# Residual rows kept in SBUF, expert weights two blocks ahead, and a last stage reordered over tiles, in a one-layer decoder step

## The chip, the cores and the metric

The kernel runs on one core of one Trainium2 chip. The metric is the device time of one execution in microseconds (us). Engines are named as the profile names them: PE (TensorE matmul), PEld (TensorE weight load, which overlaps PE), DVE (VectorE), ACT (ScalarE), POOL (GpSimd) and SP (SyncE, which here only issues transfers).

## What is computed

One decoder layer over 1,024 prompt rows, 16 meta rows and 8 sample rows (1,048 rows of 1,024 float32 values): attention and a gated recurrence are mixed, projected and added to the input, and a mixture of experts follows. Only the last part is touched by the change.

```python
x = x + (sigmoid(gm) * o_mla + sigmoid(gg) * o_gdn) @ w_out       # output projection
hf = rms_norm(x, norm_ffn)
eid, ew = hier_route(hf, w_group, b_group, w_router, b_router)    # 2 of 32 experts a row
x = x + moe_experts(hf, eid, ew, w_gate, w_up, w_down)
y = rms_norm(x, norm_final)

def moe_experts(h, expert_id, weight, w_gate, w_up, w_down):
    # rows are sorted by expert and padded to blocks of 128 slots per expert
    def expert_block(args):
        tok, e = args
        xb = h[tok]
        return (silu(xb @ w_gate[e]) * (xb @ w_up[e])) @ w_down[e]
    y = lax.map(expert_block, (slot_tok.reshape(n_blocks, 128), blk_expert))
    y = y.reshape(n_slots, -1) * slot_w[:, None]
    return zeros_like(h).at[slot_tok].add(y)
```

Each expert has w_gate and w_up of 1024x256 and w_down of 256x1024, 1 MB each. All values are float32. A matmul of float32 operands leaves two weight-load and two matmul records in the trace; a transpose leaves one of each.

## The kernel before

Stages follow each other, each a block of instruction streams for the five engines that meet only in semaphores, with a barrier between stages. The four last stages are `project_output`, `route`, `experts` and `combine`. Rows are handled in nine tiles: a first of 24 rows and eight of 128.

`project_output` (line 2139). SP issues `w_out` in two halves by output columns (`load_w`, line 2173), with the first part of the mixed activations `mix` between them (`load_mix`, line 2177), then input rows, norms, router weights and the two other parts of `mix`. For each tile PE makes 16 matmuls of 512 columns into `acc` (line 2241), DVE adds them to the rows `x` (2266), ACT squares and sums (2296), DVE and ACT make the root, DVE scales (2276) into `h`. `x` has two buffers, so POOL stores each tile of `x` to the HBM tensor `resid` (2204) and `h` to `ffn_in` (2205), and SP loads the rows of tile t+2 only after the stores of tile t (2196).

`route` (2304) computes for each row its two experts and two slots, and fills `slot_token`, the list of rows by slot. Unused slots hold token 0. It also gives `block_expert` (the expert of each block of 128 slots) and `turns`.

`experts` (2439). Blocks 0 and 1 stand before a loop of two blocks a turn, one block behind it. There are 33 blocks in use. Per block b: POOL gathers its 128 rows of `ffn_in` into `x[i]` (2531); PE turns them with eight transposes (2550), ACT and DVE copy them to `xT` (2590). For w_gate and then w_up PE makes eight matmuls (2561) with `xT` stationary (128x128) and 256 columns of weights moving; the result `gu` has slots on partitions. ACT takes silu (2604), DVE multiplies into `h` (2622), PE turns `h` with two transposes (2569), ACT copies them to `hT` (2610), and PE makes four matmuls of 512 columns with w_down (2577). ACT and DVE copy the result to `y`, which SP stores to `expert_out` (2510). PE does the transposes of block b+1 between line 2561 and line 2569 of block b. The weights have two buffers. SP issues all three transfers of block b+1 (2501 to 2503) when the w_down matmuls of block b-1 are done (`y_done`), from the start of body(b).

`combine` (2635). SP loads three tiles of `resid` ahead (2655) and one after each stored tile; POOL gathers two rows of `expert_out` per output row (2677), three tiles ahead. Per tile, in this order, DVE adds the first and second weighted rows (2688, 2690), waits for ACT's sum of squares (2706), makes mean and reciprocal (2692, 2694), waits for ACT's root (2708) and scales (2698); SP stores the tile (2665).

In rows a matmul reads "out<-moving,stationary": `ex_gu<-ex_wg,ex_xT` moves `ex_wg` through `ex_xT`.

## Time and profile before

| | us |
|---|---|
| median of 3 runs | 2903.77 (2901.22 to 2904.08) |
| the profiled execution | 2902.68 |
| its span | 2901.0 |
| project_output | about 2166 to 2332 |
| route | about 2332 to 2382 |
| experts | about 2382 to 2836 |
| combine | about 2836 to 2901 |

The profiled execution lasts 1.7 us longer than its span and lies 1.1 us under the median of the runs. Stage limits are read from the first transfers that each stage issues. Times in rows are us from the start of the span, "mean ns" is one instruction, and a bracket says how long the engine was idle before and what released it.

### The profile page before, as it was taken

How to read it: one execution, taken by the hardware profiler on the slowest of the kernel's cores; microseconds unless marked ns; L12 is line 12 of the kernel's file. 1: busy time of each engine (PE TensorE's matmuls, PEld its weight loads, DVE VectorE, ACT ScalarE, POOL GpSimd, SP SyncE). 2: the span in 40 equal slices, each digit the busy share in tenths (PEclk: the TensorE clock that was granted, in tenths of full speed). 3: DMA queues.
4: the chain of work that ended last, by engine and by line, in shares of the span. 5: the costliest groups of instructions: out<-in, count | busy, mean ns of one | idle time of the engine just before them, and what ended most of it. 6: DMA issues, size and time to landing. Idle time of an engine off the chain costs nothing. (4 is left out here: it accounts for less than half of the span.)

```text
span 2901.0 us, 45934 instructions
## 1 busy us (share of the span) xinstructions
PE 2483.2 (86%) x18544; PEld 1903.7 (66%) x18544; DVE 1151.5 (40%) x2059; ACT 852.5 (29%) x1798; POOL 654.5 (23%) x698
## 2 busy tenths in 40 slices
PE   5999999997999967499999995999969919999980
PEld 5999999997888854255655664565644516666660
DVE  6366563221566634345445552443421121111115
ACT  3257731111233320244444451343311101111111
POOL 0220000000455532232233303344400030000002
PEclk9999999998899985799999996999979959999995
DMA  4562223222633211400001005465614217888867
GB/s 128 168 215 85 79 96 118 89 83 93 192 103 107 64 39 59 159 1 23 23 31 38 23 9 197 174 258 217 243 42 169 80 65 303 318 321 332 314 265 250
DMA packets 180001, 404.16 MB, mean 139 GB/s; under 512 B 32275, under 2 KB 116984, under 8 KB 158921
## 3 DMA queue, kind: packets, MB, share of 16 engines
q1 hardware_dynamic: 144649, 245.65, 24.5%
q0 software_dynamic: 35168, 155.88, 14.8%
q8 instruction: 137, 2.24, 0.3%
q14 instruction: 47, 0.39, 0.0%
HBM read 310.76 MB, written 90.92 MB: 138 GB/s over the span
## 5 line engine op out<-in xcount | busy, mean ns | idle before, releaser
L131 PE MATMUL pi_acc<-hT_hi,pi_w_hi 128*128 128x352 f32 (+1 forms) x1152 | 378.3, 328 | 0.0
L131 PE MATMUL pi_acc<-hT_lo,pi_w_hi 128*128 128x352 f32 (+1 forms) x1152 | 371.3, 322 | 0.0
L131 PE MATMUL pi_acc<-hT_hi,pi_w_lo 128*128 128x352 f32 (+1 forms) x1152 | 371.2, 322 | 0.0
L131 PEld LDWEIGHTS pi_acc<-hT_hi,pi_w_hi 128*128 128x128 f32 x1152 | 217.2, 189 | 4.0 <-issue 3.8
L131 PEld LDWEIGHTS pi_acc<-hT_lo,pi_w_hi 128*128 128x128 f32 x1152 | 217.0, 188 | 4.0 <-issue 3.8
L131 PEld LDWEIGHTS pi_acc<-hT_hi,pi_w_lo 128*128 128x128 f32 x1152 | 216.9, 188 | 0.0
L1605 PE MATMUL at_sc<-at_keyT,at_qT 96*128 96x512 f32 (+5 forms) x480 | 162.7, 447 | 1.7 <-ACT at_val L1772 0.8
L1925 PE MATMUL as_tp<-ident,as_lat 128*128 128x128 f32 x1024 | 128.8, 281 | 25.4 <-ACT as_cT L2113 25.4
L1784 ACT ACTIVATE at_p<-at_sc,at_nm 16x16 f32<-16x16 f32 (+5 forms) x144 | 100.8, 700 | 160.0 <-DVE at_nm L1692 158.8
L1690 DVE TENSOR_REDUCE at_mx<-at_sc 16x1 f32<-16x16 f32 (+5 forms) x144 | 101.4, 704 | 99.2 <-PE at_sc L1609 98.0
L2241 PE MATMUL po_acc<-po_w,po_mix 128*128 128x512 f32 (+1 forms) x288 | 126.8, 599 | 14.0 <-DMA po_mix<-mixT 14.0
L1925 PEld LDWEIGHTS as_tp<-ident,as_lat 128*128 128x128 f32 x1024 | 113.3, 143 | 36.7 <-ACT as_cT L2113 28.9
L2577 PE MATMUL ex_yps<-ex_wd,ex_hT 128*128 128x512 f32 x264 | 122.1, 605 | 15.2 <-ACT ex_hT L2610 15.2
L2561 PE MATMUL ex_gu<-ex_wg,ex_xT 128*128 128x256 f32 x528 | 122.3, 385 | 13.5 <-DMA ex_wd<-w_down 9.7
L1623 PE MATMUL at_tp<-ident,at_p 128*128 128x128 f32 (+2 forms) x720 | 111.5, 286 | 26.1 <-ACT at_pT L1762 16.9
L2561 PEld LDWEIGHTS ex_gu<-ex_wg,ex_xT 128*128 128x128 f32 x528 | 100.0, 192 | 47.0 <-issue 34.6
L124 DVE TENSOR_SCALAR pi_m<-pi_piece 128x768 int32<-128x768 int32 (+1 forms) x72 | 40.9, 568 | 221.9 <-PE pi_acc L131 149.7
L1623 PEld LDWEIGHTS at_tp<-ident,at_p 128*128 128x128 f32 (+2 forms) x720 | 78.6, 138 | 75.4 <-issue 33.8
L651 ACT ACTIVATE pi_xr<-pi_acc 128x352 f32<-128x352 f32 x144 | 57.9, 472 | 235.4 <-PE pi_acc L131 235.4
L2113 ACT COPY as_cT<-as_tp 128x512 f32<-128x512 f32 x160 | 92.1, 586 | 98.7 <-PE as_tp L1925 98.7
L2561 PE MATMUL ex_gu<-ex_wu,ex_xT 128*128 128x256 f32 x528 | 119.3, 379 | 0.0
L1636 PE MATMUL at_op<-at_pT,at_val 128*64 128x128 f32 (+2 forms) x1440 | 114.0, 301 | 0.6 <-ACT at_pT L1762 0.6
(477 smaller groups left out, 4654.1 us busy)
## 6 DMA issues: line engine op xcount, KB each, us to landing
ex_wg<-w_gate SPq DMA_DIRECT2D x33, 1024.0 KB
ex_wu<-w_up SPq DMA_DIRECT2D x33, 1024.0 KB
ex_wd<-w_down SPq DMA_DIRECT2D x33, 1024.0 KB
pi_piece<-w_in SPq DMA_DIRECT2D x64, 384.0 KB, 3.4
expert_out<-pi_zero POOLq DMA_DIRECT2D x33, 512.0 KB, 12.0
expert_out<-ex_y SPq DMA_DIRECT2D x33, 512.0 KB, 2.7
projT<-pi_xr POOLq DMA_DIRECT2D x24, 524.0 KB, 3.0
convT<-pi_yn POOLq DMA_DIRECT2D x24, 512.0 KB, 2.9
```

What stands on the lines that cost most here:

```text
L131: last = nc.tensor.matmul(out, lhs[a], rhs[b], start=(start and i == 0), stop=(stop and i == 2))
L651: last = nc.scalar.activation(xr[:, u % XR, a0:a1], ps, func)
L1605: last = nc.tensor.matmul(scf[0:n, x:e], qT[0:QK, slot, r0:r0 + n], keyT[:, slot, x - base:e - base], start=True, stop=False, skip_group_c ...
L1623: last = nc.tensor.transpose(tp[0:kn, g % 2, j - groups[g][1], 0:n], p[0:n, u % 3, k0:k0 + kn], k.ident[0:n, 0:n])
L1636: last = nc.tensor.matmul(op[a * NOPE:(a + 1) * NOPE, 0:n], val[0:kn, j, h * NOPE:(h + 1) * NOPE], pT[0:kn, w % 2, a, j, 0:n], start=(j == ...
L1690: nc.vector.reduce_max(mx[0:n, i:i + 1], scf[0:n, base:base + kl], AX_X).then_inc(maxed, 1)
L1784: nc.scalar.activation(p[0:n, u % 3, 0:kl], scf[0:n, base:base + kl], ACT.Exp, bias=nm[0:n, i:i + 1], scale=MLA_SCALE, accum_out=l[0:n, i: ...
L1925: last = nc.tensor.transpose(tp[:, g % 3, r * P:(r + 1) * P], mine, k.ident[:])
L2113: nc.scalar.copy(cT[:, half, c, :], tp[:, g % 3, :]).then_inc(kept_a, 1)
L2241: last = nc.tensor.matmul(acc[0:n, t % 2, b, :], mix[:, c, r0:r0 + n], w[:, c, b * BANK:(b + 1) * BANK], start=(c == 0), stop=(c == KD - 1))
L2561: last = nc.tensor.matmul(gu[:, i, j, :], xT[:, i, c, :], w[:, i, c * DE:(c + 1) * DE], start=(c == 0), stop=(c == KD - 1))
L2577: last = nc.tensor.matmul(yps[:, n, :], hT[:, i, c, :], wd[:, i, c * D + n * BANK:c * D + (n + 1) * BANK], start=(c == 0), stop=(c == KE - 1))
```

## The change

- Rows of `x` stay in one SBUF tensor `resid_rows` (nine tiles, 36 KB a partition) from `project_output` to `combine`. The stores to `resid` and the loads from it are gone. The input rows of tiles 2 to 8 come in one transfer behind `mix`.
- `w_out` comes in eight parts of 512 KB (two of eight row blocks, one half of the columns), behind the first part of `mix`; tile 0 waits for them one by one.
- Unused slots of `slot_token` hold 65536. The gather gets a bound of 1047 and skips rows beyond it; the two `x` buffers are cleared by POOL first. DVE limits partition 0 of the index to 1047, so that at least one row of each block is fetched.
- In `experts` the operands of the w_gate and w_up matmuls change places: the weights are stationary, 128 of 256 columns at a time, every second one (`w[:, i, c * DE + e:(c + 1) * DE:KE]`), and the 128 slots of `xT` move. `gu` then has expert columns on partitions, DVE's product is `hT` itself, and the two transposes and ACT's copy of them are gone.
- SP issues w_gate and w_up of block b+2 when the w_gate and w_up matmuls of block b are done (`gu_done`), and w_down of block b+2 at `y_done` of block b. The expert's number is read before the wait. Two blocks stand ahead of the loop and three behind it.
- In `combine` DVE works on two tiles in turn (`normalise`, `scale`), and ACT's root comes one tile later (`root`).

PE's order in one block of `experts`, first before, then after the change; `ex_xps` are the transposes of the next block.

```order
L2561 MATMUL ex_gu<-ex_wg,ex_xT 128x256 x8
L2561 MATMUL ex_gu<-ex_wu,ex_xT 128x256 x8
L2550 MATMUL ex_xps<-ident,ex_x 128x128 x8
L2569 MATMUL ex_hps<-ident,ex_h 128x128 x2
L2577 MATMUL ex_yps<-ex_wd,ex_hT 128x512 x4
```

```order
L2568 MATMUL ex_gu<-ex_xT,ex_wg 128x128 x16
L2568 MATMUL ex_gu<-ex_xT,ex_wu 128x128 x16
L2556 MATMUL ex_xps<-ident,ex_x 128x128 x8
L2578 MATMUL ex_yps<-ex_wd,ex_hT 128x512 x4
```

Sixteen matmuls of 256 moving columns have become 32 of 128, and the line with `ex_hps` is gone.

DVE's order in `combine`, in the middle of the stage, first before, then after. `co_r` and `resid_rows` are the rows that are added to.

```order
L2688 SCALAR_TENSOR_TENSOR co_r<-co_y,weight,co_r 128x1024
L2690 SCALAR_TENSOR_TENSOR co_r<-co_y,weight,co_r 128x1024
L2692 TENSOR_SCALAR co_mean<-co_ss 128x1
L2694 RECIPROCAL co_inv<-co_mean 128x1
L2698 SCALAR_TENSOR_TENSOR co_out<-co_r,co_rstd,co_nf 128x1024
```

```order
L2690 SCALAR_TENSOR_TENSOR resid_rows<-co_y,weight,resid_rows 128x1024
L2674 TENSOR_SCALAR co_mean<-co_ss 128x1
L2676 RECIPROCAL co_inv<-co_mean 128x1
L2694 SCALAR_TENSOR_TENSOR resid_rows<-co_y,weight,resid_rows 128x1024
L2683 SCALAR_TENSOR_TENSOR co_out<-resid_rows,co_rstd,co_nf 128x1024
```

The mean, the reciprocal and the scaling now belong to the tile before the one that is being added.

The diff, cut to its core:

```diff
+NO_TOKEN = 1 << 16
...
-        x, h = s.sb("po_x", [P, 2, D]), s.sb("po_h", [P, 2, D])
+        x, h = k.resid, s.sb("po_h", [P, 2, D])
...
-                load_w(0)
                 load_mix(0)
-                load_w(1)
-                load_x(0)
-                load_x(1)
+                for i in range(4):
+                    load_w(0, i)
+                for i in range(4):
+                    load_w(1, i)
+                sp.dma_start(x[0:NS, 0, :], d["x_sample"].rearrange("b t d -> (b t) d")).then_inc(x_loaded, 16)
+                sp.dma_start(x[NS:HEAD_ROWS, 0, :], d["meta_tokens"]).then_inc(x_loaded, 16)
+                sp.dma_start(x[:, 1, :], d["x_prompt"][0, 0:P, :]).then_inc(x_loaded, 16)
...
-                for t in range(2, NT):
-                    sp.wait_ge(stored[t % 2], 32 * (t // 2))
-                    load_x(t)
+                sp.dma_start(x[:, 2:, :], d["x_prompt"][0, P:, :].rearrange("(t p) n -> p t n", p=P)).then_inc(rows_loaded, 16)
...
-                    pool.dma_start(d["resid"][r0:r0 + n, :], x[0:n, t % 2, :]).then_inc(stored[t % 2], 16)
                     pool.dma_start(d["ffn_in"][r0:r0 + n, :], h[0:n, t % 2, :]).then_inc(stored[t % 2], 16)
...
-                        if t == 0:
-                            pe.wait_ge(w_loaded[b], 16)
                         for c in range(KD):
+                            if t == 0 and c % 2 == 0:
+                                pe.wait_ge(w_loaded[b][c // 2], 16)
...
-                    dve.wait_ge(x_loaded[i], 16 * (t // 2 + 1) + (16 if i == 0 else 0))
+                    if t < 2:
+                        dve.wait_ge(x_loaded, 48)
+                    else:
+                        dve.wait_ge(rows_loaded, 16)
...
-                nc.gpsimd.memset(zero[:], 0).then_inc(cleared, 1)
+                nc.gpsimd.memset(zero[:], NO_TOKEN).then_inc(cleared, 1)
...
-                link(V.tensor_scalar(k.turns[:], incl[0:1, EXPERTS - 1:EXPERTS], -2.0, None, ALU.add))
+                link(V.tensor_scalar(k.turns[:], incl[0:1, EXPERTS - 1:EXPERTS], -4.0, None, ALU.add))
...
+            more = eng.value_load(k.turns[0:1, 0:1], min_val=(2 * ROWS // P - 4) // 2, max_val=TURNS)
+            body(0, 0, 2)
+            body(1, 1, 2)
             with eng.Fori(0, TURNS) as i:
-                with eng.If(i < busy):
-                    body(i * 2 + 2, 0, False)
-                    body(i * 2 + 3, 1, False)
-            body(busy * 2 + 2, 0, True)
-            return busy
+                with eng.If(i < more):
+                    body(i * 2 + 2, 0, 2)
+                    body(i * 2 + 3, 1, 2)
+            body(more * 2 + 2, 0, 2)
+            body(more * 2 + 3, 1, 1)
+            body(more * 2 + 4, 0, 0)
+            return more
...
-                def load(b, i):
-                    if not fixed(b) or b >= 2:
-                        sp.wait_ge(y_done, b - 1)
+                def load(b, i, before):
+                    e = sp.value_load(k.block_expert[0:1, bass.ds(b, 1)], min_val=0, max_val=EXPERTS - 1)
+                    if before is not None:
+                        sp.wait_ge(gu_done, before + 1)
                         sp.sem_inc(load_due, 1)
-                    e = sp.value_load(k.block_expert[0:1, bass.ds(b, 1)], min_val=0, max_val=EXPERTS - 1)
                     sp.dma_start(wg[:, i, :], wg_d[bass.ds(e, 1)].rearrange("e p n -> p (e n)")).then_inc(w_loaded[i], 16)
                     sp.dma_start(wu[:, i, :], wu_d[bass.ds(e, 1)].rearrange("e p n -> p (e n)")).then_inc(w_loaded[i], 16)
+                    if before is not None:
+                        sp.wait_ge(y_done, before + 1)
+                        sp.sem_inc(load_due, 1)
                     sp.dma_start(wd[:, i, :], wd_d[bass.ds(e, 1)].rearrange("e p n -> p (e n)")).then_inc(w_loaded[i], 16)
 
-                def body(b, i, last_one):
-                    if not last_one:
-                        load(b + 1, 1 - i)
+                def body(b, i, ahead):
+                    if ahead > 1:
+                        load(b + 2, i, b)
                     sp.wait_ge(y_kept_a, b + 1)
                     sp.wait_ge(y_kept_v, b + 1)
                     sp.dma_start(d["expert_out"][bass.ds(b * P, P), :], y[:, i].rearrange("p b n -> p (b n)")).then_inc(stored[i], 16)
 
...
+                load(0, 0, None)
+                load(1, 1, None)
+                more = turns(sp, body)
...
                     pool.sem_inc(gather_due, 1)
                     nc.gpsimd.indirect_dma_start(out=x[i][:], out_offset=None, in_=d["ffn_in"],
-                                                 in_offset=bass.IndirectOffsetOnAxis(ap=idx[i][:, 0:1], axis=0)).then_inc(gathered[i], 16)
+                                                 in_offset=bass.IndirectOffsetOnAxis(ap=idx[i][:, 0:1], axis=0),
+                                                 bounds_check=ROWS - 1, oob_is_err=False).then_inc(gathered[i], 16)
...
+                for i in range(2):
+                    nc.gpsimd.memset(x[i][:], 0.0).then_inc(x_cleared, 1)
+                pool.wait_ge(x_cleared, 2)
                 pool.wait_ge(slots_kept, 2)
...
                     for j, w in enumerate((wg, wu)):
-                        for c in range(KD):
-                            last = nc.tensor.matmul(gu[:, i, j, :], xT[:, i, c, :], w[:, i, c * DE:(c + 1) * DE], start=(c == 0), stop=(c == KD - 1))
+                        for e in range(KE):
+                            for c in range(KD):
+                                last = nc.tensor.matmul(gu[:, i, j, e * P:(e + 1) * P], w[:, i, c * DE + e:(c + 1) * DE:KE], xT[:, i, c, :], start=(c == 0), stop=(c == KD - 1))
                     last.then_inc(gu_done, 1)
-                    if not last_one:
+                    if ahead:
                         turn(b + 1, 1 - i)
                     pe.wait_ge(h_done, b + 1)
-                    if not fixed(b) or b >= 1:
-                        pe.wait_ge(h_kept, b)
-                    for c in range(KE):
-                        last = nc.tensor.transpose(hps[:, c, :], h[:, i, c:DE:KE], k.ident[:])
-                    last.then_inc(h_turned, 1)
-                    pe.wait_ge(h_kept, b + 1)
                     if not fixed(b) or b >= 1:
...
-                    act.wait_ge(h_turned, b + 1)
-                    if not fixed(b) or b >= 2:
-                        act.wait_ge(y_done, b - 1)
-                    nc.scalar.copy(hT[:, i], hps[:]).then_inc(h_kept, 1)
...
                     if not fixed(b) or b >= 2:
-                        dve.wait_ge(h_turned, b - 1)
-                    nc.vector.tensor_tensor(h[:, i, :], act_g[:, i, :], gu[:, i, 1, :], ALU.mult).then_inc(h_done, 1)
-                    if not last_one:
+                        dve.wait_ge(y_done, b - 1)
+                    nc.vector.tensor_tensor(hT[:, i].rearrange("p c t -> p (c t)"), act_g[:, i, :], gu[:, i, 1, :], ALU.mult).then_inc(h_done, 1)
...
-                nc.vector.tensor_copy(idx_all[:], hps[:, 0, 0:BLOCKS]).then_inc(slots_kept, 1)
+                nc.vector.tensor_copy(idx_all[:], hps[:, 0, 0:BLOCKS]).then_inc(idx_turned, 1)
+                dve.wait_ge(idx_turned, 1)
+                nc.vector.tensor_scalar(idx_all[0:1], hps[0:1, 0, 0:BLOCKS], float(ROWS - 1), None, ALU.min).then_inc(slots_kept, 1)
...
-        r, out = s.sb("co_r", [P, 3, D]), s.sb("co_out", [P, 3, D])
+        r, out = k.resid, s.sb("co_out", [P, 3, D])
...
-                def load(t):
-                    r0, n = TILES[t]
-                    sp.dma_start(r[0:n, t % 3, :], d["resid"][r0:r0 + n, :]).then_inc(r_loaded[t % 3], 16)
-
-                load(0)
-                load(1)
-                load(2)
...
-                    if t + 3 < NT:
-                        load(t + 3)
...
+                def normalise(t):
+                    i, n = t % 3, TILES[t][1]
                     dve.wait_ge(squared, t + 1)
                     nc.vector.tensor_scalar(mean[0:n, t:t + 1], ss[0:n, t:t + 1], 1.0 / D, EPS, ALU.mult, ALU.add).then_inc(meaned, 1)
                     dve.wait_ge(meaned, t + 1)
                     nc.vector.reciprocal(inv[0:n, t:t + 1], mean[0:n, t:t + 1]).then_inc(inverted, 1)
+
+                def scale(t):
+                    i, n = t % 3, TILES[t][1]
                     dve.wait_ge(rooted, t + 1)
                     if t >= 3:
                         dve.wait_ge(stored[i], 16 * (t // 3))
-                    nc.vector.scalar_tensor_tensor(out=out[0:n, i, :], in0=rt, scalar=rstd[0:n, t:t + 1], in1=nf[0:n, :], op0=ALU.mult, op1=ALU.mult).then_inc(normed, 1)
+                    nc.vector.scalar_tensor_tensor(out=out[0:n, i, :], in0=r[0:n, t, :], scalar=rstd[0:n, t:t + 1], in1=nf[0:n, :], op0=ALU.mult, op1=ALU.mult).then_inc(normed, 1)
+
+                dve.wait_ge(nf_loaded, 16)
+                for t, (r0, n) in enumerate(TILES):
+                    i = t % 3
+                    dve.wait_ge(gathered[i], 32 * (t // 3 + 1))
+                    rt = r[0:n, t, :]
+                    nc.vector.scalar_tensor_tensor(out=rt, in0=y[0][i][0:n, :], scalar=k.weight[0:n, 0, t:t + 1], in1=rt, op0=ALU.mult, op1=ALU.add).then_inc(half, 1)
+                    if t:
+                        normalise(t - 1)
+                    dve.wait_ge(half, t + 1)
+                    nc.vector.scalar_tensor_tensor(out=rt, in0=y[1][i][0:n, :], scalar=k.weight[0:n, 1, t:t + 1], in1=rt, op0=ALU.mult, op1=ALU.add).then_inc(added, 1)
+                    if t:
+                        scale(t - 1)
+                normalise(NT - 1)
+                scale(NT - 1)
...
                 for t, (r0, n) in enumerate(TILES):
+                    if t:
+                        root(t - 1)
                     act.wait_ge(added, t + 1)
...
-                    nc.scalar.activation(square[0:n, :], r[0:n, t % 3, :], ACT.Square, accum_out=ss[0:n, t:t + 1]).then_inc(squared, 1)
-                    act.wait_ge(inverted, t + 1)
-                    nc.scalar.activation(rstd[0:n, t:t + 1], inv[0:n, t:t + 1], ACT.Sqrt).then_inc(rooted, 1)
+                    nc.scalar.activation(square[0:n, :], r[0:n, t, :], ACT.Square, accum_out=ss[0:n, t:t + 1]).then_inc(squared, 1)
+                root(NT - 1)
...
+        k.resid = k.sb("resid_rows", [P, NT, D])
```

## Rows read from the trace of the kernel before

**Rows 1.** Window over experts: us; busy us (count) per engine; PEclk, DMA share, GB/s
```profile
2397.00:2832.00 435.00, 400.86 (x1642) 291.38 (x1642) 58.64 (x99) 64.05 (x133) 35.72 (x62) 1.00 0.78 306
```

**Rows 2.** Timeline of one block of experts: start us, us, engine, line, operation
```profile
2597.96 3.62 PE L2561 MATMUL ex_gu<-ex_wu,ex_xT 128*128 128x256 f32 x16
...
2601.41 1.05 PE L2550 MATMUL ex_xps<-ident,ex_x 128*128 128x128 f32 x8
...
2602.03 0.42 DVE L2622 TENSOR_TENSOR ex_h<-ex_act_g,ex_gu 128x256 f32<-128x256 f32 x1 [7.43 <-ACT ex_act_g L2604]
...
2602.51 0.51 PE L2569 MATMUL ex_hps<-ident,ex_h 128*128 128x128 f32 x2
...
2603.47 3.70 PE L2577 MATMUL ex_yps<-ex_wd,ex_hT 128*128 128x512 f32 x8 [0.46 <-ACT ex_hT L2610]
...
2607.01 3.62 PE L2561 MATMUL ex_gu<-ex_wg,ex_xT 128*128 128x256 f32 x16
```

**Rows 3.** Timeline, PE in experts: the same later, and its first and last block
```profile
2397.79 2.47 PE L2561 MATMUL ex_gu<-ex_wg,ex_xT 128*128 128x256 f32 x5 [0.88 <-DVE ex_xT L2590]
...
2610.46 3.62 PE L2561 MATMUL ex_gu<-ex_wu,ex_xT 128*128 128x256 f32 x16
...
2620.47 3.69 PE L2561 MATMUL ex_gu<-ex_wg,ex_xT 128*128 128x256 f32 x16 [0.63 <-DMA ex_wd<-w_down]
...
2818.64 3.71 PE L2561 MATMUL ex_gu<-ex_wg,ex_xT 128*128 128x256 f32 x16 [2.93 <-issue]
```

**Rows 4.** 128-column matmuls (timeline, x16); weight loads by line: ns min/median/max
```profile
821.77 1.95 PE L853 MATMUL gp_i<-gp_heads 128*128 128x128 f32 x16
...
L853 PEld LDWEIGHTS gp_i<-gp_heads x128: 190/192/192, 739.3 to 1018.2; 128*128 128x128 f32 x128
...
L844 PEld LDWEIGHTS gp_r<-ident,gp_heads x64: 139/141/146, 738.5 to 1016.4; 128*128 128x128 f32 x64
...
L2550 PEld LDWEIGHTS ex_xps<-ident,ex_x x264: 186/190/226, 2394.9 to 2810.6; 128*128 128x128 f32 x132
```

**Rows 5.** Waits in experts (us in total, times, longest); window at full DMA load
```profile
PE ex_gu L2561 <- DMA ex_wd<-w_down: 9.0, 14, 0.9
...
SPq L2509 <- DVE ex_y L2596: 336.9, 33, 25.0
...
2598.00:2603.00 5.00, 4.95 (x27) 4.17 (x25) 0.93 (x2) 0.89 (x2) 0.18 (x1) 1.00 0.99 415
```

**Rows 6.** Timeline of combine: first and last tile, and one in the middle on DVE
```profile
2845.69 1.27 DVE L2688 SCALAR_TENSOR_TENSOR co_r<-co_y,weight,co_r 24x1024 f32<-24x1024 f32 x1 [13.29 <-DMA co_y<-expert_out,dest]
...
2869.10 1.28 DVE L2688 SCALAR_TENSOR_TENSOR co_r<-co_y,weight,co_r 128x1024 f32<-128x1024 f32 x1
2870.42 1.28 DVE L2690 SCALAR_TENSOR_TENSOR co_r<-co_y,weight,co_r 128x1024 f32<-128x1024 f32 x1
...
2872.92 0.15 DVE L2692 TENSOR_SCALAR co_mean<-co_ss 128x1 f32<-128x1 f32 x1 [1.22 <-ACT co_square L2706]
...
2873.54 1.28 DVE L2698 SCALAR_TENSOR_TENSOR co_out<-co_r,co_rstd,co_nf 128x1024 f32<-128x1024 f32 x1 [0.27 <-ACT co_rstd L2708]
2874.74 1.28 DVE L2688 SCALAR_TENSOR_TENSOR co_r<-co_y,weight,co_r 128x1024 f32<-128x1024 f32 x1
...
2891.65 1.28 DVE L2688 SCALAR_TENSOR_TENSOR co_r<-co_y,weight,co_r 128x1024 f32<-128x1024 f32 x1
```

**Rows 7.** Windows: combine at its start and in its middle
```profile
2838.00:2845.00 7.00, 0.00 (x0) 0.00 (x0) 0.00 (x0) 0.00 (x0) 4.73 (x6) 0.50 0.99 284
2845.00:2880.00 35.00, 0.00 (x0) 0.00 (x0) 24.07 (x30) 9.39 (x19) 11.36 (x12) 0.50 0.92 328
```

**Rows 8.** Timeline and window of the start of project_output
```profile
2166.05 0.37 SPq L2175 DMA_DIRECT2D po_w<-w_out  x1
...
2175.92 16.56 PE L2241 MATMUL po_acc<-po_w,po_mix 128*24 128x512 f32 x34 [13.98 <-DMA po_mix<-mixT]
...
2170.00:2174.00 4.00, 0.00 (x0) 0.00 (x0) 0.00 (x0) 0.00 (x0) 0.00 (x0) 0.50 1.06 386
```

78 lines of the change are left out of this document (31 added, 47 removed).

## The prediction

> **What bounds the kernel now.** I read windows first to see which engine is full in which stage, then the timeline of one block or tile, then waits. The change touches three stages. In `experts` PE is busy 401 of 435 us at full clock, the transfers 0.78 of the time at 306 GB/s [rows 1], so PE and the chain that it waits for come first and transfers second. One block [rows 2]: from the w_up matmuls at 2597.96 to those of the next block at 2610.46 [rows 3] are 12.50 us. In them PE stands still only around the turning of `h`: 2602.51 the two transposes, 2603.47 the w_down matmuls, 0.96 us. Every second block is longer, since w_down of the next block has not landed: 9.0 us in 14 waits [rows 5], and 13.46 us from the start at 2607.01 to that at 2620.47. Over all blocks it is (2818.64 - 2397.79) / 32 = 13.15 us [rows 3]. In `combine` the chain DVE, ACT, DVE of each tile sets the pace: 5.64 us from 2869.10 to 2874.74 [rows 6], with transfers at 0.92 of the time and 328 GB/s [rows 7], so that they are not far behind. At the start of `project_output` PE waits 13.98 us, the last 9.87 of them for transfers issued from 2166.05 on [rows 8].
>
> The sum is made against the profiled execution, 2902.68 us, which is 1.1 us under the median of the runs; I add that at the end.
>
> **project_output.** Before, the first matmul needs 2 MB of w_out and 0.62 MB of mix. At the 386 GB/s of [rows 8] that is 7.0 of the 9.87 us, so 2.8 us are latency. After, it needs 0.62 + 0.52 MB: 3.0 + 2.8 = 5.8 us, 4 us earlier. The seven other parts take 1.4 us each; PE makes 34 matmul records in 16.56 us [rows 8], 0.49 us each, four to a part, so it asks for a part every 1.9 us and never waits. The rest of the stage is PE's, so the 4 us last to its end. The rows of tiles 2 to 8 (3.7 MB) stand last in SP's queue, behind some 9.6 MB: 34 us in all. DVE needs them when tile 2 is made, three tiles of 32 x 0.49 = 15.6 us after the first matmul, so they cost nothing. Bounds: 3 to 5. The smaller stores of POOL and the missing waits of SP cost and give nothing: DVE waits there for PE.
>
> **experts, the matmuls turned round.** Before, 32 records of 256 columns: 3.45 us for 16 [rows 2, 3], 0.216 each, 6.90 a block. After, 64 records of 128 columns, each with its own weight load. The nearest rows are contiguous float32 matmuls of this shape: 16 in 1.95 us [rows 4], the eight transposes in 1.05 us [rows 2], so eight more cost 0.90, 0.112 each. 64 x 0.112 = 7.17, 0.27 us more a block. This is the term on which all hangs, for the new stationary operand is read with a step of two elements, and no row has a float32 weight load with both its records at a step. What there is [rows 4]: contiguous loads last 192 ns for matmuls and 141 for transposes; the transposes of `ex_x`, read with a step of eight, 190. So a step costs a transpose 50 ns, and takes it to what a matmul's load has anyway. Two readings: a step only takes away something that transposes have and matmuls do not (spacing stays 0.112), or it doubles every load (spacing 0.215). I take the first, since 190 and 192 ns look like one floor, and the stepped transposes still follow each other at 0.11 us. The second is a rival.
>
> The Trainium skill, "SBUF — State Buffer", section "Door 1: The DMA port swizzle", says that SBUF has lines of 16 bytes and float32 can be read with a step of up to four elements at full rate. By that rule the load at a step of two costs nothing and the sum stays. No row here has that step on a weight load of a matmul, and a step of eight, which the rule charges, shows 190 against 141 ns.
>
> **experts, the chain.** Before, the last w_up matmul starts at 2597.96 + 15 x 0.216 = 2601.20, and the transposes of `h` 1.31 us later, released by DVE's product, which ends at 2602.45 [rows 2]. After, w_down's matmuls start there, and 0.11 earlier since the last matmul is 0.27 and not 0.38 us long: 1.20 us, of which the transposes of `x` fill 0.9. The 0.96 us for turning and copying `h` go. Next, w_down to the next block: 2607.01 - 2603.47 = 3.54, unchanged. A block: 63 x 0.112 + 1.20 + 3.54 = 11.80 us, 0.70 less than 12.50.
>
> **experts, weights two ahead.** The need per block is 3.1 MB of weights, 0.26 to 0.52 of gathered rows and 0.52 stored, 4.1 MB at most. At the 415 GB/s of a full window [rows 5] that is 9.9 us of 11.80, and each load has a whole block of slack, so the 0.88 us of every second block go (on average 0.44). SP's waits: the store of `y` now stands behind the wait for `y_done`, which comes before `y_kept` anyway, and the next w_gate stands behind the store; SP waits 336.9 us in this stage [rows 5], so nobody waits for it. The gather stands behind PE's transposes of the block before as it did, nine us ahead of its use.
>
> Sum: the first interval keeps its 1.6 us of half clock, the last its 3.1 us of empty loop turns (2.93 idle at 2818.64 [rows 3]). 31 intervals of 11.80, one of 14.9, plus 1.6 = 382.3, against 420.9 before: 38.6 less. The last block gives 0.7. The start: the first gather may be shorter by half, POOL's clears lie in its wait for the slot list, DVE's extra operation costs 0.2: 0 to 2, I take 0.7. Together 40 us, bounds 34 (a spacing of 0.115, a tenth of the blocks stalled) and 43.
>
> **combine.** First tile: 1.15 MB of `resid` no longer lie ahead of the gathers; at 284 GB/s [rows 7] 4.0 us, I take 3.5, since latency stays (0 to 4). Then DVE's work a tile: from the scaling to the next addition 1.20 (2873.54 to 2874.74), from addition to mean the same 1.20, mean and reciprocal 0.35, the second addition 1.24: 4.0 us against 5.64 [rows 6]. The wait of 1.22 us for the sum of squares and ACT's root now lie under other operations of DVE, the first addition and the second. What is late next is the transfers: 1.57 MB a tile, at 328 / 0.92 = 357 GB/s [rows 7] 4.4 us. Three tiles lie ready at the start, so I take 4.3. Eight intervals: 45.96 before (2845.69 to 2891.65 [rows 6]), 34.4 after, 11.6 less; with the start 15.1. The first of the eight intervals has no scaling and no mean in it yet, 2.6 us of DVE's work instead of 4.0; transfers allow about 1 us of that, so I take 16. Bounds: 8 (transfers at 328 GB/s, no gain at the start) and 19.
>
> **Sum.** 4 + 40 + 16 = 60: 2902.7 - 60 = 2842.7, and 1.1 for the median: **2844 us**.
>
> **The rivals.**
> - A, the sum above. Its own range is 2837 to 2856.
> - B, slower: the stepped weight load doubles. 64 records at 0.215 instead of 0.112 add 6.6 us a block, 33 blocks 218 us: 3062 us. It decides where the spacing passes 0.112 + 60 / 2112 = 0.140 us. For it speaks that a step visibly lengthens transposes' loads; against it, that the length ends at the matmul's own. Spacings between (0.16) give 2945.
> - C, transfers take the place of the chain: gathers, issued just after 2 MB of w_gate and w_up, land late, or w_down does. PE then waits as now, and blocks fall back to about 12.5 us: 31 x 0.7 = 22 us given back, 2866. For it: 9.9 of 11.8 us leaves little, and `combine` shows what mixed queues do to the rate (284 against 415 GB/s). Against: the slack of a whole block.
> - D, the change does not do what it says: the loads two ahead bring nothing because SP issues them late, blocks stay at alternating lengths. 31 x 0.44 = 14 us less gain, 2858. It falls in with C.
> - E, no difference. It needs a loss of 60 us at one place that is not B; I see none but a spacing near 0.14.
>
> **How the numbers follow.** A 0.70, B with its spacings between 0.14, C and D 0.12, faster than A (transfers lighter than I count, a start without waiting) 0.03, E 0.01. A measurement of this kernel can tell some 0.2%, 5.8 us, from no change. Faster by more than that: A, C, D and the faster case, 0.85. Slower: B, 0.14. Same: 0.01. The range takes in A, C, D and most of the faster case, 2832 to 2870; B, the other sign, lies outside with 0.14.
>
> **What would show each step.** Spacing of the records of `ex_gu`: 32 in about 3.6 us, or 6.9 in case B. Start of w_down's matmuls 1.2 us after the last of w_up, no wait on a copy of `hT`. Starts of w_gate's matmuls 11.8 us apart with no alternation and no wait on `ex_wd`; a wait on `ex_x` would be C. In `combine` 4.0 to 4.4 us between scalings on DVE; a wait on `co_y` means that transfers bind. First matmul of `project_output` 5.8 us after SP's first issue; a DVE wait on the rows of tiles 2 to 8 would break that step. The prediction is wrong at its root if the weight loads, 64 a block, last much more than 192 ns.

## The result and the profile after

The changed kernel takes 2858.52 us (median of 4 executions, 2857.41 to 2868.63) beside 2903.88 us for the kernel before on the same chip: a ratio of 0.9854, 95% interval 0.9831 to 0.9877. The forecast was 2844 us, range 2832 to 2870. The profiled execution took 2859.27 us with a span of 2857.6. That is 43.4 us less than before, where the sum of the prediction had 60.

To find where they went I cut each profiled execution at three marks: SyncE's first issue of `project_output`, the first w_gate matmul of `experts`, and SyncE's issue of `co_nf`, with which `combine` begins. Timeline of after at the three marks, with the row of before that has no group above:

```profile
2165.75 0.36 SPq L2174 DMA_DIRECT2D po_mix<-mixT  x1
...
2171.68 3.58 PE L2234 MATMUL po_acc<-po_w,po_mix 128*24 128x512 f32 x4 [10.05 <-DMA po_w<-w_out]
...
2393.36 5.65 PE L2568 MATMUL ex_gu<-ex_xT,ex_wg 128*128 128x128 f32 x32 [0.87 <-DVE ex_xT L2591]
...
2808.55 0.35 SPq L2650 DMA_DIRECT2D co_nf<-norm_final  x1
```

```profile
2836.35 0.35 SPq L2651 DMA_DIRECT2D co_nf<-norm_final  x1
```

| stage, us | before | after | gain | forecast |
|---|---|---|---|---|
| up to `project_output` (code unchanged) | 2166.05 | 2165.75 | 0.3 | 0 |
| `project_output`, `route`, to the first w_gate matmul | 231.74 | 227.61 | 4.1 | 4 + 0.7 |
| `experts`, to the issue of `co_nf` | 438.56 | 415.19 | 23.4 | 39.3 |
| `combine`, to the end | 64.65 | 49.05 | 15.6 | 16 |

Three of four stages came out as forecast; `experts` gave 15.9 us less. The total alone would not tell case A from rival D, which had 2858 us; the rows of `experts` do. One block of it in the timeline of after, to be read against [rows 2, 3], and the next start:

```profile
2554.20 3.92 PE L2568 MATMUL ex_gu<-ex_xT,ex_wg 128*128 128x128 f32 x32
2557.96 3.93 PE L2568 MATMUL ex_gu<-ex_xT,ex_wu 128*128 128x128 f32 x32
2561.73 1.04 PE L2556 MATMUL ex_xps<-ident,ex_x 128*128 128x128 f32 x8
2562.82 3.70 PE L2578 MATMUL ex_yps<-ex_wd,ex_hT 128*128 128x512 f32 x8
2566.36 3.92 PE L2568 MATMUL ex_gu<-ex_xT,ex_wg 128*128 128x128 f32 x32
2570.12 3.93 PE L2568 MATMUL ex_gu<-ex_xT,ex_wu 128*128 128x128 f32 x32
2573.89 1.04 PE L2556 MATMUL ex_xps<-ident,ex_x 128*128 128x128 f32 x8
2575.15 3.70 PE L2578 MATMUL ex_yps<-ex_wd,ex_hT 128*128 128x512 f32 x8 [0.22 <-DVE ex_hT L2619]
```

The reader is to see three things. Nothing waits for `ex_wd` any more. The 32 matmul records of w_gate take 2557.96 - 2554.20 = 3.76 us, 0.1175 us each and not 0.112. And the step from the transposes of `x` to w_down's matmuls is 1.09 us in one block and 1.26 in the next, so that starts of w_gate lie 12.16 and 12.33 us apart in turn, where 11.80 was forecast. The other differences are at the end of the loop. Timeline of after there, and windows. The first window is from the middle of the stage and has the busy time of all engines, as in [rows 1]; the other two have that of PE alone, then PEclk, DMA share and GB/s:

```profile
2765.37 5.56 PE L2568 MATMUL ex_gu<-ex_xT,ex_wg 128*128 128x128 f32 x32 [2.96 <-issue]
2770.76 3.93 PE L2568 MATMUL ex_gu<-ex_xT,ex_wu 128*128 128x128 f32 x32
```

```profile
2500.00:2600.00 100.00, 98.69 (x654) 81.65 (x654) 15.12 (x26) 13.31 (x26) 9.83 (x17) 1.00 0.90 323
...
2762.00:2766.00 4.00, 1.04 (x5) 0.96 1.01 335
2766.00:2770.00 4.00, 4.00 (x24) 0.61 0.88 308
```

The empty turns of the loop cost 2.96 us, as before the change (2.93, [rows 3]). But the w_gate matmuls behind them now take 5.56 us instead of 3.92, at a mean granted clock of 0.61 of 2.4 GHz, which is part of the time at 1.2 GHz. Before the change the same pause left the clock alone: 3.71 us [rows 3].

### The profile page after: what moved, and what is told of

The parts are those of the page before. It is cut to its first block and busy times, and to the rows that moved or that the text cites. A ratio compares the mean times of both kernels' runs of the same rounds, so it can differ in the third digit from the quotient of the medians.

```text
span 2857.6 us, 47826 instructions
## 1 busy us (share of the span) xinstructions
PE 2481.4 (87%) x19534; PEld 1940.6 (68%) x19534; DVE 1149.9 (40%) x2060; ACT 840.9 (29%) x1765; POOL 660.0 (23%) x691
## 5 line engine op out<-in xcount | busy, mean ns | idle before, releaser
L2568 PEld LDWEIGHTS ex_gu<-ex_xT,ex_wg 128*128 128x128 f32 x1056 | 132.6, 201 | 19.7 <-issue 19.7
L2568 PE MATMUL ex_gu<-ex_xT,ex_wg 128*128 128x128 f32 x1056 | 132.8, 286 | 3.8 <-issue 3.0
L1624 PE MATMUL at_tp<-ident,at_p 128*128 128x128 f32 (+2 forms) x720 | 111.5, 286 | 26.1 <-ACT at_pT L1763 16.9
L2568 PE MATMUL ex_gu<-ex_xT,ex_wu 128*128 128x128 f32 x1056 | 129.8, 281 | 0.0
L2568 PEld LDWEIGHTS ex_gu<-ex_xT,ex_wu 128*128 128x128 f32 x1056 | 127.0, 197 | 0.0
```

Of the source, the lines that this page charges most:

```text
L1624: last = nc.tensor.transpose(tp[0:kn, g % 2, j - groups[g][1], 0:n], p[0:n, u % 3, k0:k0 + kn], k.ident[0:n, 0:n])
L2568: last = nc.tensor.matmul(gu[:, i, j, e * P:(e + 1) * P], w[:, i, c * DE + e:(c + 1) * DE:KE], xT[:, i, c, :], start=(c == 0), stop=(c == ...
```

## Experiments

A table first, since it is what most of the runs are read by. All are profiled executions, cut at the same marks.

| run | up to `project_output` | to first w_gate | `experts` | `combine` | intervals of w_gate's starts |
|---|---|---|---|---|---|
| before | 2166.05 | 231.74 | 438.56 | 64.65 | 12.58 / 13.46 |
| after | 2165.75 | 227.61 | 415.19 | 49.05 | 12.16 / 12.33 |
| c2 contiguous slices | 2167.97 | 226.67 | 401.37 | 49.29 | 11.77 / 11.94 |
| c4 weights moving | 2168.44 | 228.08 | 426.55 | 49.83 | 12.50 / 12.67 |
| c5 loads one ahead | 2161.37 | 227.71 | 433.76 | 50.56 | 12.25 / 13.5 |
| c6 all rows gathered | 2165.60 | 227.63 | 415.31 | 51.36 | 12.16 / 12.32 |
| c7 combine in order | 2159.85 | 227.76 | 415.01 | 60.68 | 12.16 / 12.33 |
| c8 w_out in halves | 2165.00 | 231.45 | 415.07 | 47.78 | 12.16 / 12.32 |
| c9 loop to `more` | 2164.32 | 227.68 | 410.38 | 50.32 | 12.16 / 12.32 |
| c10 = c2 + c9 | 2162.12 | 226.43 | 398.54 | 50.41 | 11.77 / 11.94 |
| c11 = c10, waits, buffers | 2166.42 | 226.48 | 399.97 | 46.33 | 11.84 / 11.97 |
| c13 = c10, buffers | 2166.14 | 226.83 | 398.36 | 46.57 | 11.77 / 11.94 |

The first column is the same code in every row and differs by up to 8.6 us. `experts` has the same code in after, c7 and c8, and takes 415.01 to 415.19 us. So there a stage's own time resolves tenths of a microsecond where the whole resolves three or four, and where `experts` answers the question, I go by it. `combine` does not resolve as well: with the changed order and three buffers it takes 47.78 to 51.36 us in eight of these rows. Its gain of 15.6 us, from one execution of each kernel, could as well have been read as 13.3 to 16.9.

### c2: contiguous stationary slices

My theory of the missing 15.9 us: the weight loads of w_gate and w_up, read at every second element, are slower. The rival: matmuls are slowed by the transfers that now run beside all of them. To keep the result right the edit also lays w_down out anew, in two pieces of 4 KB per partition in place of one of 8 KB.

```
-wd_d = d["w_down"][0].rearrange("e (p c) n -> e p (c n)", p=P)
+wd_d = d["w_down"][0].rearrange("e (c p) n -> e p c n", p=P)
...
-  w[:, i, c * DE + e:(c + 1) * DE:KE]
+  w[:, i, c * DE + e * P:c * DE + (e + 1) * P]
```

> Stationary slices of w_gate and w_up contiguous (columns e*128 to e*128+127 of each chunk) instead of every second element; w_down is rearranged to match (row c*128+p, two pieces of 4 KB per partition instead of one of 8 KB), so the result is unchanged. Theory (the missing gain of the experts is the step of two): records of w_gate and w_up come 0.112 us apart instead of 0.118, the weight-load record takes 0.192 instead of 0.197, the interval between blocks falls from a mean of 12.25 to about 11.9, and the whole by 33 x 0.37 = 12 us, to about 2846. Rival (the matmuls are slowed by the transfers that now run beside all of them): spacing stays at 0.117 to 0.118 and the time at 2858. A second rival: 4 KB pieces make the w_down transfer later and a wait on ex_wd comes back, intervals 12.5 or more, 2865 or slower.

Measured: 2845.53 us, ratio 0.9814, interval 0.98 to 0.9828. Timeline of c2, a w_gate and a w_up pass, and the w_gate pass behind the pause:

```profile
2408.65 3.73 PE L2568 MATMUL ex_gu<-ex_xT,ex_wg 128*128 128x128 f32 x32
2412.22 3.74 PE L2568 MATMUL ex_gu<-ex_xT,ex_wu 128*128 128x128 f32 x32
...
2755.53 3.83 PE L2568 MATMUL ex_gu<-ex_xT,ex_wg 128*128 128x128 f32 x32 [2.92 <-issue]
```

3.57 us for 32, 0.112 each, exactly what the contiguous rows of [rows 4] had given; the transfers run beside as before (from 2500 to 2600 us at 336 GB/s and a share of 0.94, in after 323 and 0.90). The trace of after settles the rival too, and with it the other half of the edit. In its last block the passes are as long as in the middle, 3.76 us from w_gate's start to w_up's and 3.93 us for w_up's records, although no weights are being loaded any more: the queues move 131 GB/s from 2791 to 2795 us and nothing from 2795 to 2799. Timeline of after:

```profile
2791.49 3.92 PE L2568 MATMUL ex_gu<-ex_xT,ex_wg 128*128 128x128 f32 x32
2795.25 3.93 PE L2568 MATMUL ex_gu<-ex_xT,ex_wu 128*128 128x128 f32 x32
```

The weight loads by line, after first, then c2 (columns: busy us, mean ns):

```profile
L2568 PEld LDWEIGHTS ex_gu<-ex_xT,ex_wu 128*128 128x128 f32 x384 | 46.2, 197 | 0.0
```

```profile
L2568 PEld LDWEIGHTS ex_gu<-ex_xT,ex_wu 128*128 128x128 f32 x384 | 43.8, 192 | 0.0
```

197 ns against 192. The theory held, the rival is out: 0.39 us a block, 12.3 us in all. The other 1.5 of the 13.8 us by which `experts` is shorter in c2 is the pass behind the pause, 3.83 us where after had 5.56. The second rival, a late w_down in smaller pieces, did not come either.

### c3 and c12: steps of eight and of four

```
-  w[:, i, c * DE + e:(c + 1) * DE:KE]
+  w[:, i, e * 1024 + c:(e + 1) * 1024:8]
```

> Stationary slices of w_gate and w_up taken at every 8th element (32 bytes) instead of every 2nd; the values multiplied are then not the right columns, all else is unchanged. If a stepped weight load costs more as the step grows (the rival of the prediction by which a load doubles once it spans more lines of memory), spacing goes from 0.118 to 0.2 or more and the time from 2858 to 3030 or more; at the level of a load of twice the length (0.215) 33 x 64 x 0.097 = 205 us, 3063. If only being stepped at all costs, whatever the step, spacing stays 0.118 and the time 2858.

> Stationary slices of w_gate and w_up taken at every 4th element (16 bytes) instead of every 2nd; the values multiplied are then not the right columns, all else is unchanged. Steps of 1, 2 and 8 gave spacings of 0.112, 0.118 and 0.240 us. If a load is free up to a step of four elements (the rule of 16-byte lines as the Trainium skill has it) and only 0.006 us above a contiguous one as at two, spacing is 0.118 and the time 2858. If its cost grows with the span of memory that it covers, spacing lies between, near 0.15 to 0.18: 33 x 64 x 0.03 to 0.06 = 65 to 130 us more, 2920 to 2985.

(c12 differs from c3 in the step alone, 4 in place of 8.) Timelines, c3 first, then c12:

```profile
2511.75 7.69 PE L2568 MATMUL ex_gu<-ex_xT,ex_wg 128*128 128x128 f32 x32
2519.27 5.92 PE L2568 MATMUL ex_gu<-ex_xT,ex_wu 128*128 128x128 f32 x24
```

```profile
2512.37 7.50 PE L2568 MATMUL ex_gu<-ex_xT,ex_wg 128*128 128x128 f32 x32
2519.71 5.53 PE L2568 MATMUL ex_gu<-ex_xT,ex_wu 128*128 128x128 f32 x23
```

| step, elements (bytes) | us per record | whole, us |
|---|---|---|
| 1 (4) | 0.112 | 2846 |
| 2 (8) | 0.1175 | 2859 |
| 4 (16) | 0.229 | 3097 |
| 8 (32) | 0.235 | 3109 |

For eight I had given two outcomes without choosing, and the doubled one came, 46 us above its 3063. For four I had 0.118 or 0.15 to 0.18, and neither came. It is not the clock: from 2500 to 2600 us it was granted at 1.00 in both, and no wait for a transfer stands in either stage. The load records last 338 ns at a step of eight and 330 at four (median), against 197 at two and 192 contiguous. The cost does not grow in proportion to the span. It jumps to double between a step of two and one of four, and barely moves after that. So rival B, the doubled load, is real; this kernel stands one doubling of the step short of it, with two elements of every 16 bytes in use. A step of three was not run. One execution each is enough for 240 us.

### c4 and c5: the two halves of the change in experts

c4 turns the orientation back (w_gate and w_up moving, `h` transposed and copied) and keeps the loads two ahead; c5 does the reverse.

```
 c4:
-  last = nc.tensor.matmul(gu[:, i, j, e * P:(e + 1) * P], w[:, i, c * DE + e:(c + 1) * DE:KE], xT[:, i, c, :], ...)
+  last = nc.tensor.matmul(gu[:, i, j, :], xT[:, i, c, :], w[:, i, c * DE:(c + 1) * DE], ...)
 ...
+  last = nc.tensor.transpose(hps[:, c, :], h[:, i, c:DE:KE], k.ident[:])
 c5:
-  if ahead > 1: load(b + 2, i, b)
+  if ahead: load(b + 1, 1 - i)
```

> The changed kernel with the orientation of w_gate and w_up as before the change (weights moving, x stationary, h turned by two transposes and one copy), everything else of the change kept, loads two ahead too. Theory (terms add): no wait on ex_wd any more, interval 12.50 to 12.58 in every block, so the experts take 32 x 0.1 to 0.3 = 3 to 10 us more than in the changed kernel: 2862 to 2869. So the loads ahead are worth about 18 to 20 us and turning only 4 to 9. Rival (the loads ahead bring little, the turned orientation carried the gain): waits on ex_wd stay, intervals 12.6 / 13.4, 2885.

> The changed kernel with the weight loads one block ahead, as before the change (SyncE's order and waits of before), turned orientation and everything else kept. Theory: every second block waits for ex_wd again; the block that waits keeps its interval near 13.4 because the transfers set it and the other takes 12.2, mean 12.8, 32 x 0.55 = 18 us more than the changed kernel: 2876; if the pair of blocks is set by its transfers alone (26.0 for two), 13.0 and 2882. Rival (the loads ahead are worth nothing, since the halved gather freed the queues): no wait on ex_wd, intervals 12.2, 2858.

Measured: c4 2868.45 us, ratio 0.9888 (0.9873 to 0.9903); c5 2875.5 us, ratio 0.9919 (0.9904 to 0.9934). Both totals are within what the theory gave. The stage of c4 is not: its `experts` took 11.4 us more than in after, where the theory had 3 to 10, so turning is worth more beside early loads than I had put it. Timeline of c5, a block that waits, and waits of PE from 2410 to 2750 us (us in total, times, longest), in c5 and in after:

```profile
2507.16 4.01 PE L2564 MATMUL ex_gu<-ex_xT,ex_wg 128*128 128x128 f32 x32 [1.01 <-DMA ex_wd<-w_down]
...
PE ex_gu L2564 <- DMA ex_wd<-w_down: 14.2, 14, 1.3
```

```profile
PE ex_yps L2578 <- DVE ex_hT L2619: 3.1, 14, 0.2
```

| `experts`, us | loads one ahead | loads two ahead |
|---|---|---|
| weights moving | 438.56 | 426.55 |
| turned, step of two | 433.76 | 415.19 |
| turned, contiguous | not run | 401.37 |

The two halves do not add. Alone, turning brings 4.8 us and the loads 12.0; together 23.4. The reason stands in the waits: with loads one ahead a wait on `ex_wd` grew on average from 0.64 us (9.0 in 14 waits, [rows 5]) to 1.01 (14.2 in 14), so what PE saved in a waiting block went into the wait.

### c6: gathering all rows

```
-nc.gpsimd.memset(zero[:], NO_TOKEN)
+nc.gpsimd.memset(zero[:], 0)
...
-  bounds_check=ROWS - 1, oob_is_err=False
```

> The changed kernel, but empty slots of a block gather row 0 again instead of being skipped (slot list cleared with 0, no bounds on the gather), so the gathered bytes are those of before the change. Theory (the halved gather only makes transfers lighter, PE sets the interval): the experts move 0.25 MB more per block of 12.25 us, 21 GB/s on top of 323 at a share of 0.90; that stays under the full 359 GB/s (323 / 0.90), so intervals stay at 12.16 and 12.33 and the time at 2858 to 2860. Rival (the queues were just kept off the path by the smaller gather): waits on ex_wd or ex_x return, intervals 12.6 or more, 2870.

Measured: 2859.05 us, ratio 0.9848 (0.9824 to 0.9872). Windows of c6 in the middle of the stage:

```profile
2500.00:2600.00 100.00, 98.69 (x655) 81.68 (x654) 15.09 (x26) 13.28 (x26) 9.38 (x17) 1.00 0.95 341
```

`experts` takes 415.31 us instead of 415.19. Skipping empty slots brings the share from 0.95 to 0.90 and no time. The start gained nothing by it either: the first gather lands 9.1 us after its issue before and after the change (2381.45 to 2390.55).

### c7 and c8: combine in order, w_out in halves

```
 c7:
-  if t: normalise(t - 1)
...
-  if t: scale(t - 1)
+  normalise(t)
+  scale(t)
 c8:
-  load_mix(0)
-  for i in range(4): load_w(0, i)
-  for i in range(4): load_w(1, i)
+  load_half(0)
+  load_mix(0)
+  load_half(1)
```

> The changed kernel with VectorE's and ScalarE's order in combine as before the change (each tile is added, normalised and scaled before the next), rows still kept on chip. Theory: the start keeps its 4.3 us, the tile period goes back from 3.9 to 5.64, so of the 15.6 us of this stage 11 to 12 are lost: 2869 to 2871. Rival (the gain of the stage came from the residual loads that no longer share the queues, and transfers set the period): period 4.4 or less, 2862 or faster.

> The changed kernel with w_out loaded in two halves and mix between them as before the change, rows still kept on chip. Theory: first matmul of project_output 9.9 us after SyncE's first issue instead of 5.9, 4 us later, and all after it: 2862.5. Rival (the four microseconds are given back, since VectorE or the stores of ffn_in set the end of the stage): 2858.5.

Measured: c7 2870.42 us, ratio 0.9892 (0.9876 to 0.9908); c8 2860.69 us, ratio 0.9857 (0.9841 to 0.9873). VectorE's additions in `combine`, timeline of c7, first tile, two in the middle, last tile:

```profile
2807.56 1.27 DVE L2690 SCALAR_TENSOR_TENSOR resid_rows<-co_y,weight,resid_rows 24x1024 f32<-24x1024 f32 x1 [8.85 <-DMA co_y<-expert_out,dest]
...
2830.97 1.28 DVE L2690 SCALAR_TENSOR_TENSOR resid_rows<-co_y,weight,resid_rows 128x1024 f32<-128x1024 f32 x1
...
2836.61 1.28 DVE L2690 SCALAR_TENSOR_TENSOR resid_rows<-co_y,weight,resid_rows 128x1024 f32<-128x1024 f32 x1
...
2853.52 1.28 DVE L2690 SCALAR_TENSOR_TENSOR resid_rows<-co_y,weight,resid_rows 128x1024 f32<-128x1024 f32 x1
```

Timeline of after, the first four tiles, two that wait, and the last:

```profile
2813.63 1.27 DVE L2690 SCALAR_TENSOR_TENSOR resid_rows<-co_y,weight,resid_rows 24x1024 f32<-24x1024 f32 x1 [9.00 <-DMA co_y<-expert_out,dest]
...
2818.21 1.28 DVE L2690 SCALAR_TENSOR_TENSOR resid_rows<-co_y,weight,resid_rows 128x1024 f32<-128x1024 f32 x1 [1.99 <-DMA co_y<-expert_out,dest]
...
2822.18 1.28 DVE L2690 SCALAR_TENSOR_TENSOR resid_rows<-co_y,weight,resid_rows 128x1024 f32<-128x1024 f32 x1
...
2826.02 1.28 DVE L2690 SCALAR_TENSOR_TENSOR resid_rows<-co_y,weight,resid_rows 128x1024 f32<-128x1024 f32 x1
...
2835.18 1.28 DVE L2690 SCALAR_TENSOR_TENSOR resid_rows<-co_y,weight,resid_rows 128x1024 f32<-128x1024 f32 x1 [1.41 <-DMA co_y<-expert_out,dest]
...
2840.01 1.28 DVE L2690 SCALAR_TENSOR_TENSOR resid_rows<-co_y,weight,resid_rows 128x1024 f32<-128x1024 f32 x1 [0.91 <-DMA co_y<-expert_out,dest]
...
2847.69 1.28 DVE L2690 SCALAR_TENSOR_TENSOR resid_rows<-co_y,weight,resid_rows 128x1024 f32<-128x1024 f32 x1
```

In c7 the eight intervals sum to 2853.52 - 2807.56 = 45.96 us, to the hundredth those of before [rows 6], with no residual loads in the queues: they had cost nothing but the start (the first addition of c7 comes 4.94 us after the issue of `co_nf`). In after the intervals sum to 34.06. So of the 15.6 us, 4.3 are the first tile (5.08 us after the issue of `co_nf` instead of 9.34) and 11.9 the order of VectorE's work; 0.6 is given back behind the last addition.

c8: the stage up to the first w_gate takes 3.84 us longer, the first matmul comes 9.84 us after SyncE's first issue instead of 5.93. The four microseconds are there and reach the experts; its `combine` was the shortest of those with three buffers, so the total, 2.2 us above after's where 4 were expected, shows them only in part.

### c9 and c10: the loop ends where the work does

```
-with eng.Fori(0, TURNS) as i:
-    with eng.If(i < more):
+with eng.Fori(0, more) as i:
```

> The changed kernel with the loop over pairs of blocks ending at the computed number of turns, in place of a loop of the largest number with an If inside; the result is the same for any routing. Theory: the 2.96 us in which TensorE waits for the empty turns go, and the slow pass after them with it (granted clock 0.61, 1.6 us): 2854 to 2855.5. The alternation of the intervals, 12.16 and 12.33, then tells of its cause: if it is the If and the branch around the pair, it goes too and the time is 2851.5; if not, it stays.

> Contiguous stationary slices together with the loop that ends at the computed number of turns, all else as in the changed kernel. Theory (the two gains add, since both are TensorE's own time on the path): intervals 11.77 and 11.94 throughout, no pause at the end of the loop; experts 12 + 4.8 us shorter than in the changed kernel, 2842. Rival (TensorE now asks for weights faster than they land): waits on ex_wg, ex_wu or ex_wd appear and the interval stays over 12: 2846 or slower.

Measured: c9 2853.93 us, ratio 0.9834 (0.982 to 0.9849), `experts` 4.8 us shorter: 2.96 of the pause, 1.6 of the slow pass, 0.2 unplaced. The alternation stays, so it is not the If. c10 2839.2 us, ratio 0.979 (0.9771 to 0.9808), with `experts` at 398.54 us, and still no wait on any weight. Its `experts` are 16.7 us shorter than after's, where the theory had 16.8. It beats both kernels: 62 us less than before, some 19 less than the changed one.

### c11 and c13: order of waits, buffers for all gathers

In after's trace ScalarE's silu starts 0.20 us after the first transpose of `x` in the block of 2561.73, and 0.27 in that of 2573.89; VectorE's product follows it by 0.41 and 0.51 us. That makes the 0.17 us of the alternation. My explanation, which the views do not show, since register operations are not in them: the expression `b - 1` of a wait met long ago is computed after the late wait. c11 puts the old wait first on the three engines; c11 and c13 give each of `combine`'s 18 gathers its own buffer.

```
-act.wait_ge(gu_done, b + 1)
 if not fixed(b) or b >= 2: act.wait_ge(h_done, b - 1)
+act.wait_ge(gu_done, b + 1)
...
-if t >= 3: pool.wait_ge(added, t - 2)
```

> The kernel of the run before this one (contiguous slices, loop to the computed number) with two more edits in separate stages. In experts the wait that was met long ago is put ahead of the one that is late, on ScalarE (h_done of the block before last ahead of gu_done), on VectorE and on TensorE: in the changed kernel's trace ScalarE's and VectorE's products start 0.08 us later in every second block, each behind a register operation that stands between the two waits. Theory: the alternation of 0.17 us goes and all intervals are 11.77 or a little less, 16 x 0.17 = 2.7 us. Rival: it comes from something else (the bank of PSUM, the loop), intervals stay 11.77 and 11.94. In combine every tile's two gathers have buffers of their own, so GpSimd issues all 18 without waiting for an addition. Theory: VectorE's three waits for co_y (1.99, 1.41, 0.91 us) shrink, 1 to 4 us from the first issue of the stage to its end, which then takes 45 to 48 instead of 49 us. Rival: transfers at 370 GB/s are the bound, and the stores queue behind the gathers, 49 us or more. In all 2835 to 2840.

> Contiguous slices, loop to the computed number of turns, and a buffer of its own for each of the 18 gathers of combine; the order of the waits as in the changed kernel. Theory (the reordered waits cost 0.04 us a block and the separate gather buffers bring 3 us in combine, two effects in separate stages): experts again with intervals 11.77 and 11.94 and 398.5 us from its first w_gate matmul to the first issue of combine, instead of 400.0, and combine 46.3 us instead of 50.4; span 2834 to 2836, median 2836. Rival (the 46.3 us of one execution was chance): combine 49 to 50 us, 2839.

Measured: c11 2840.21 us, ratio 0.9781 (0.9764 to 0.9799); c13 2839.57 us, ratio 0.979 (0.9773 to 0.9807). Neither can be told from c10 in the whole, and c13's total is the one that its rival had; up to `project_output` it took 4.0 us more than c10. By stages: w_down's matmuls in c11, timeline, with the transposes ahead of them:

```profile
2556.93 1.05 PE L2555 MATMUL ex_xps<-ident,ex_x 128*128 128x128 f32 x8
2558.24 3.67 PE L2577 MATMUL ex_yps<-ex_wd,ex_hT 128*128 128x512 f32 x8 [0.27 <-DVE ex_hT L2618]
...
2568.89 1.05 PE L2555 MATMUL ex_xps<-ident,ex_x 128*128 128x128 f32 x8
2570.08 3.67 PE L2577 MATMUL ex_yps<-ex_wd,ex_hT 128*128 128x512 f32 x8
```

1.31 and 1.19 us, where c10 has 1.26 and 1.09. The edit to the waits failed: both kinds of block got later, `experts` took 1.4 us more. But the slow block is now the odd one, where it was the even one, and in c13, which has the old order, it is the even one again. So the order of the waits bears on the alternation; that it alone makes it is not shown, and how to be rid of it stays open. In `combine` the buffers work: 46.33 and 46.57 us, against 47.78 to 51.36 in the other eight runs of the table that keep the changed order of `combine` with three buffers (mean 49.8), some three microseconds, and 1.2 to 1.5 even against the shortest. What VectorE still waits for `co_y` in c13 behind its first tile is 2.26 us at the second and 0.33 later.

## Why the prediction was right, and where not

The time lay in the range and the mechanism was that of case A, but 14.5 us above the forecast and 2.5 above case A's own range. In part that was luck: the argument by which A was taken before B does not hold, as the second point says.

- **project_output, -4.** Right: 3.84 by c8, the first matmul 5.93 us after the first issue, forecast 5.8. The rows of tiles 2 to 8 never show as a wait. VectorE's first addition waits for `po_br`, under PE's work.
- **Matmuls turned round: this term was mis-sized.** The step put the record spacing at 0.112, by reading equal loads of 190 and 192 ns as a floor that a step cannot raise. It is 0.1175: 64 times 0.0055 to 0.006, 0.35 to 0.39 us a block, 12.3 us in all. The row I leaned on, transposes read with a step of eight at 190 ns [rows 4], was the wrong neighbour. In c3 those transposes still load at that pace (188 ns), while a matmul's weights at the same step of eight load in 338 and take 0.235 us a record. The transpose's row did not carry over to a matmul's load. Bounds for this term reached to 0.115 only, and for the rest relied on rival B; the runs show B's size (0.215 forecast, 0.229 and 0.235 measured) nearly right, for steps of four and eight. The argument from one floor made no difference between steps. At a step of eight, the very step it was read from, it would have been wrong by some 250 us; it held here because this kernel's step is two.
- **The rule I weighed.** By this kernel's runs a float32 weight load is near full speed at a step of two (0.1175 against 0.112) and at half speed at four (0.229). The Trainium skill, "SBUF — State Buffer", section "Door 1: The DMA port swizzle", has lines of 16 bytes that want at least two hits each, and from this a free step of up to four float32. Its first half agrees with the jump; the second does not, and the measurement decides: of the steps run here (one, two, four, eight) two is the last cheap one.
- **The chain.** Right in the fast blocks: w_gate to w_gate 11.77 us with contiguous slices, forecast 11.80. In every second block 0.17 us more, 2.7 us in all, which no row that I had read showed: in before it lies under the stalls. c4, with the old orientation and no stalls, has it too, 12.50 and 12.67.
- **Weights two ahead.** Right: no wait for `ex_wd` is left, so rivals C and D did not come, although D's number, 2858, did. The forecast split, 0.70 and 0.44 us a block, held only for both together, as c4 and c5 show.
- **The loop's end.** I kept 3.1 us for the pause and had nothing for the clock behind it: 1.6 us more.
- **The start, -0.7.** It gave 0.3 (231.74 to c8's 231.45); the gather did not become quicker.
- **combine, -16.** Right, 15.6, as far as one execution of each kernel can tell, in its parts too: 4.3 at the start (3.5), 11.9 in the intervals (12.5 with the first one's extra), 0.6 back at the end. The transfers were as close as forecast: VectorE ran at 3.84 us a tile, under my 4.3, then waited 1.41 and 0.91 us for `co_y`.

In `experts` 39.3 was forecast and 23.4 came. The gap of 15.9 is 12.3 of spacing, 2.7 of alternation and 1.6 behind the pause, less 0.9 since the fast block is 0.03 us under my 11.80; 0.2 is left unplaced. In c2, without the spacing and the slow pass, the stage takes 401.4 us, where the sum had 399.3; the 2.1 us between them are the alternation less the quicker fast block. c10 comes to 398.5, below the sum, only because the pause of 3.1 us that the sum kept is gone too.

## What to carry to other kernels

Before a matrix becomes the stationary operand, look at the step at which its columns are read: with float32 weights here, steps of one and two are nearly alike (0.112 and 0.1175 us a record), four and eight double it (0.229 and 0.235), and a rearranged load elsewhere (here two pieces of 4 KB for w_down) may buy the step of one for nothing. An engine's saving and a transfer's saving on the same path need not add (4.8 and 12.0 us alone, 23.4 together): value them together, or one of them will seem worth little. Cut executions at marks and compare stages; parts worth 3 to 4 us could be sized here only that way. Look first how much each stage differs among kernels that share its code: `experts` 0.2 us, `combine` 3.6.

## What I had not expected of the hardware

- The clock behind a pause. TensorE stood still for 2.9 us at the same place in several kernels. The pass after it took 5.56 us in after (granted clock 0.61 from 2766 to 2770 us), the same 5.56 in c6, c7 and c8, which share its w_gate and w_up code, and 5.40 in c4; in before it took 3.71, in c2 3.83 and in c5 4.03, within 0.11 us of the usual. The transfers do not part the two groups: c2 ran at 349 GB/s behind its pause and before at 4. What decides it stays open. Timeline of c4:

```profile
2778.70 5.40 PE L2567 MATMUL ex_gu<-ex_wg,ex_xT 128*128 128x256 f32 x16 [2.92 <-issue]
```

- GpSimd's issue of a gather in `combine` took 0.95 us mostly, and in after 1.75 us each of the five times when it began right behind a wait for VectorE. Neither the wait nor VectorE's work beside it explains this alone. In before and in c7 the gathers wait for VectorE too, but VectorE then stands idle for 1.2 us, and they take 0.94 or 0.95. In c11 they wait for nothing beside the same work of VectorE, and most take 0.94. Both together gave 1.75 (once 2.94, in c8), and a few without a wait were long as well (1.71 and 1.89 in after, 2.08 in c11). The cause stays open. Timeline of after, GpSimd:

```profile
2825.17 1.75 POOL L2666 DMA_INDIRECT co_y<-expert_out,dest  x1 [0.89 <-DVE resid_rows L2694]
...
2827.23 0.94 POOL L2666 DMA_INDIRECT co_y<-expert_out,dest  x1 [0.30 <-issue]
```

- With w_down loaded in pieces of 4 KB (c2, c10, c11, c13) the first gather landed 7.8 to 8.2 us after its issue, with 8 KB pieces 9.0 to 9.3 us, and the stage before the experts is about a microsecond shorter. Shorter pieces ahead of it in the queues may be the reason; that was not tested.
